# Hybrid encoder on one core: gate fills ahead of the attention units, and weights split in the projection

## The reference, cut to what matters

```
h = x @ W_in                        # one projection: q, k, v, gates of all branches, latents
A: causal attention with a forget term      logit[t,s] += F[t] - F[s]
B: window of 128 keys, one learned sink per head
C: keys and values from a normed latent     q = norm(cq) @ W_uq, k = ckv @ W_uk, v = ckv @ W_uv
branch_n = (attention_n * silu(gate_n)) @ W_br[n]            # "up"
m = sum over n of sigmoid(g_n) * branch_n                    # g = x @ W_in[:, 3072 gate columns]
x = LayerNorm(alpha * x + m @ W_o)
```

## Time and profile before

| | |
|---|---|
| median of the runs | 3636.93 us |
| profiled execution | 3634.75 us, of which the span is 3633.1 |
| TensorE busy | 3259.5 us, 90% |
| VectorE, ScalarE, GpSimd busy | 40%, 25%, 5% |
| granted TensorE clock, mean | 0.961 of full speed |
| DMA, mean | 116 GB/s |

### The profile page before, as it was taken

How to read it: one execution, slowest core, us unless ns; L and a number is a source line. 1 busy time by engine, 2 the same in 40 slices (tenths; PEclk the granted TensorE clock), 3 DMA queues, 4 the chain that set the end, 5 groups by cost and what they waited for, 6 DMA issues and landing times. The chain is left out here.

```text
span 3633.1 us, 52418 instructions
## 1 busy us (share of the span) xinstructions
PE 3259.5 (90%) x20718; PEld 2656.5 (73%) x20718; DVE 1466.5 (40%) x3367; ACT 896.6 (25%) x2006; POOL 172.6 (5%) x118
## 2 busy tenths in 40 slices
PE   0999986999999997988969999779999999977988
PEld 0788886777777775667858888767787777745867
DVE  5214234444444442354631143444434444423556
ACT  0221212333223332220121212223332233322110
POOL 0000000100110100000000000010111110000000
PEclk9999998999999998989979999889999999987999
DMA  5322216322333216764342222352223232096633
GB/s 197 110 87 94 84 54 201 86 69 59 88 93 88 83 39 173 228 234 151 127 157 89 91 96 68 115 158 68 69 72 91 85 94 66 30 262 205 217 136 110
DMA packets 405163, 419.73 MB, mean 116 GB/s; under 512 B 154561, under 2 KB 314177, under 8 KB 402561
## 3 DMA queue, kind: packets, MB, share of 16 engines
q1 hardware_dynamic: 371088, 376.87, 33.5%
q10 hardware_dynamic: 33840, 39.66, 3.3%
HBM read 291.17 MB, written 127.64 MB: 115 GB/s over the span
## 5 line engine op out<-in xcount | busy, mean ns | idle before, releaser
L351 PE MATMUL proj_acc<-proj_wh,keep_xh 128*128 128x512 f32 (+1 forms) x1296 | 501.7, 387 | 12.5 <-DVE proj_wl L326 12.5
L1066 PE MATMUL att_gacc<-att_gwh,keep_xh 128*128 128x256 f32 x1728 | 504.6, 292 | 2.5 <-POOL att_gwl L986 2.5
L352 PE MATMUL proj_acc<-proj_wl,keep_xh 128*128 128x512 f32 (+1 forms) x1296 | 500.4, 386 | 0.0
L353 PE MATMUL proj_acc<-proj_wh,keep_xl 128*128 128x512 f32 (+1 forms) x1296 | 500.2, 386 | 0.0
L1068 PE MATMUL att_gacc<-att_gwh,keep_xl 128*128 128x256 f32 x1728 | 486.8, 282 | 0.0
L1067 PE MATMUL att_gacc<-att_gwl,keep_xh 128*128 128x256 f32 x1728 | 485.9, 281 | 0.0
L1150 DVE COPY att_pt<-att_tr 128x256 f32<-128x256 f32 (+3 forms) x384 | 177.2, 461 | 620.9 <-PE att_tr L1031 620.6
L1093 ACT ACTIVATE att_p<-att_ss,att_stat 128x257 f32<-128x257 f32 (+9 forms) x384 | 249.4, 650 | 691.5 <-DVE att_stat L1143 691.5
L1020 PE MATMUL att_ss<-att_kt,att_qt 64*128 64x256 f32 (+9 forms) x1024 | 376.2, 469 | 1.3 <-DVE att_kt L1078 1.3
L1066 PEld LDWEIGHTS att_gacc<-att_gwh,keep_xh 128*128 128x128 f32 x1728 | 326.5, 189 | 17.2 <-issue 10.6
L1067 PEld LDWEIGHTS att_gacc<-att_gwl,keep_xh 128*128 128x128 f32 x1728 | 326.2, 189 | 0.0
(11 more groups left out here) (294 smaller groups left out, 4393.5 us busy)
## 6 DMA issues: line engine op xcount, KB each, us to landing
scratch_gates<-att_gout SPq DMA_DIRECT2D x216, 128.0 KB, 1.7
up_gates<-scratch_gates SPq DMA_DIRECT2D x18, 1536.0 KB, 8.0
proj_raw<-in_w_in SPq DMA_DIRECT2D x48, 512.0 KB, 3.7
att_graw<-in_w_in SPq DMA_DIRECT2D x48, 512.0 KB, 3.7
str_ka<-in_cache_a_kT SPq DMA_DIRECT2D x16, 1024.0 KB, 9.7
str_va<-in_cache_a_v SPq DMA_DIRECT2D x16, 1024.0 KB, 5.4
scratch_sg<-proj_out SPq DMA_DIRECT2D x54, 256.0 KB, 2.0
att_sg<-scratch_sg SPq DMA_DIRECT2D x24, 512.0 KB, 6.0
```

The lines of the kernel that those rows point to most:

```text
L351: nc.tensor.matmul(bank, hi, wh[:, u, kt, 0:w], start=kt == 0, stop=False)
L352: nc.tensor.matmul(bank, hi, wl[:, u, kt, 0:w], start=False, stop=False)
L353: mm = nc.tensor.matmul(bank, lo, wh[:, u, kt, 0:w], start=False, stop=kt == KT - 1)
L1066: nc.tensor.matmul(gacc[:, 0:GW], hi, gwh[:, n % 2, k, :], start=k == 0, stop=False)
```

## The change

The split weights of gate group 0 are made in the projection stage and kept (`keep_gw0`); its fills 0 to 3 are formed at the opening of the latent stage; the list of all fills runs on in one sequence, so fills 4 to 6 of group 0 open the attention, and units 0 to 6 have no fill at sub 13. A kept tile `early` of three row tiles serves in turn the x rows (ring of three), the raw gate weights, the position tables, `wq`, and the first rows of the up weights. The four row tiles of the attention's first unit are loaded in the latent stage, into a kept tile `row`.

```diff
+GW = 256
+EARLY_FILLS = 4
 # projections
-    XA = 4
+    XA = EARLIEST            # 3
+    graw = [C["early"][:, half, :] ... for half in range(2)]
 # SyncE, over the chunks c
+                if c in (1, 2):
+                    sp.dma_start(graw[half], w_src[... O_GATE:O_GATE + GW]).then_inc(gw_loaded, 16)
+                if c == 3:
+                    sp.wait_ge(gw_lo, 2)
+                    sp.dma_start(rope, ...); sp.dma_start(ropec, ...)
 # GpSimd
+            pool.wait_ge(x_taken, 2 * NT)
+            for half in range(2):
+                pool.wait_ge(gw_loaded, 16 * (half + 1))
+                nc.gpsimd.tensor_copy(hi, graw[half]).then_inc(gw_hi, 1)
+                nc.gpsimd.tensor_tensor(lo, graw[half], hi.bitcast(F32), ALU.subtract).then_inc(gw_lo, 1)
 # ScalarE
-            act.dma_start(rope[:], ...)
-            act.dma_start(ropec[:], ...)
 # latent_keys, SyncE, behind the first latent rows and wq
+            for i in range(RING):
+                sp.dma_start(C["row"][:, i, :, 0:HD], ...).then_inc(first_loaded, 16)
+            for t in range(EARLY_FILLS):
+                sp.wait_ge(g_taken, t + 1)
+                sp.dma_start(S["gates"][rows(t), 0:GW], gout[:, t, :]).then_inc(g_stored, 16)
 # TensorE, ahead of turn(0)
+            for t in range(EARLY_FILLS):
+                for k in range(KT):
+                    ...  # three matmuls into gacc[t]
 # ScalarE
+            take_gates(range(2))
+            act.wait_ge(wq_loaded, 16)
+            for raw, hi, lo in splits[:KQ]: ...
+            take_gates(range(2, EARLY_FILLS))
             take_turned(0)
 # VectorE
-            low_turned(0)
             for i, (raw, hi, lo) in enumerate(splits):
+                if i == KQ:
+                    low_turned(0)
 # attention_order
-    fills = [2, 3, 4, 5, 6, 8, 10, 12, 13]
+    fills = [(n, t) for n in range(len(UNITS)) for t in range(NT)][EARLY_FILLS:]
+    order = [("fill", *fills.pop(0)) for _ in range(3)] + order
+    places = [2, 3, 4, 5, 6, 8, 10, 12, 13]
+    spare = EARLY_FILLS + 3
-            if m in fills:
-                order.append(("fill", n, fills.index(m)))
+            if m in (places[:-1] if n < spare else places):
+                order.append(("fill", *fills.pop(0)))
 # prompt_attention, SyncE
-            load_row(0) ... load_gate(0, 0) ... load_gate(0, 1)
+            load_gate(1, 0) ... load_gate(1, 1)
+            sp.dma_start(C["early"][:], w_br_tiles(T, l)[:, 0:EARLIEST, :]).then_inc(early_loaded, 16)
-                    if t == 0 and n + 1 < len(UNITS):
+                    if t == 0 and 1 <= n and n + 1 < len(UNITS):
                         load_gate(n + 1, 0)
-                    if t == NT - 1 and n + 1 < len(UNITS):
+                    if t == NT - 1 and 1 <= n and n + 1 < len(UNITS):
                         load_gate(n + 1, 1)
 # the gate tiles sgr and sgt have one buffer each, before two
```

More of the change, by code:

```diff
@@ L256, in projections @@
     gkv = ph.sb("gkv", [P, KR])
-    XA = 4
-    xrow = ph.sb("xrow", [P, XA, D])
+    XA = EARLIEST
+    xrow = C["early"]
+    flat = C["early"][:].rearrange("p k n -> p (k n)")
+    rope = flat[:, 0:NT * 128].rearrange("p (t c) -> p t c", t=NT)
+    ropec = flat[:, NT * 128:NT * 192].rearrange("p (t c) -> p t c", t=NT)
+    graw = [C["early"][:, half, :].rearrange("p (k n) -> p k n", k=KT // 2) for half in range(2)]
+    gw_loaded, gw_hi, gw_lo = ph.sem("gw_loaded"), ph.sem("gw_hi"), ph.sem("gw_lo")
     x_loaded, x_taken = ph.ring("x_loaded", XA), ph.sem("x_taken")
@@ L327, in split_lo, with _ @@
                                     wh[:, u, kt, 0:w].bitcast(F32), ALU.subtract).then_inc(w_ready[u], 1)
+        @block.gpsimd
+        def _(pool):
+            pool.wait_ge(x_taken, 2 * NT)
+            for half in range(2):
+                hi, lo = (C["gw0"][:, r, 4 * half:4 * half + 4] for r in range(2))
+                pool.wait_ge(gw_loaded, 16 * (half + 1))
+                nc.gpsimd.tensor_copy(hi, graw[half]).then_inc(gw_hi, 1)
+                pool.wait_ge(gw_hi, half + 1)
+                nc.gpsimd.tensor_tensor(lo, graw[half], hi.bitcast(F32), ALU.subtract).then_inc(gw_lo, 1)
+            pool.wait_ge(gw_lo, 2)
         @block.tensor
@@ L577, in latent_keys @@
         ph.sem(n) for n in ("q_taken", "q_out", "k_taken", "k_out", "v_out"))
-    stored = ph.ring("stored", 2)
+    stored, first_loaded = ph.ring("stored", 2), ph.sem("first_loaded")
     HQ = H // 2
@@ L657, in forget_sums @@
                 mm.then_inc(sums_made, 1)
+            for t in range(EARLY_FILLS):
+                for k in range(KT):
+                    hi, lo = (x[:, k, rows(t)] for x in (C["xh"], C["xl"]))
+                    wh, wl = (C["gw0"][:, r, k, :] for r in range(2))
+                    nc.tensor.matmul(gacc[t], hi, wh, start=k == 0, stop=False)
+                    nc.tensor.matmul(gacc[t], hi, wl, start=False, stop=False)
+                    mm = nc.tensor.matmul(gacc[t], lo, wh, start=False, stop=k == KT - 1)
+                mm.then_inc(g_made, 1)
             turn(0)
@@ L826, in attention_order @@
     order += [("gate", len(UNITS) - 1, PT - 1), ("mix", len(UNITS) - 1, PT - 1)]
+    assert not fills
     return order
@@ L862, in prompt_attention, with gate_weights, fill_of @@
     g_made, g_taken, g_stored = ph.sem("g_made"), ph.sem("g_taken"), ph.ring("g_stored", 3)
+    def gate_weights(n):
+        return ((C["gw0"], gw1)[n % 2][:, r] for r in range(2))
+    def fill_of(n, t):
+        return NT * n + t - EARLY_FILLS
     groups = {}
@@ L970, in _ @@
             for part in range(3):
-                sp.wait_ge(g_stored[part], 16 * 3 * len(UNITS))
+                sp.wait_ge(g_stored[part], 16 * len(range(EARLY_FILLS + (part - EARLY_FILLS) % 3, NT * len(UNITS), 3)))
         @block.gpsimd
@@ L1309, in _ @@
                 load_c(n)
[L1310 removed]
+            sp.dma_start(C["early2"][:], w_br_tiles(T, l)[:, EARLIEST:EARLY, :]).then_inc(early_loaded, 16)
             def place(name, tile, h, wanted):
@@ L1711, in stream_attention, with early_tile @@
     ph.end()
-EARLY = 6
+EARLIEST, EARLY = 3, 6
+def early_tile(C, k):
+    return C["early"][:, k, :] if k < EARLIEST else C["early2"][:, k - EARLIEST, :]
 def w_br_tiles(T, l):
@@ L1732, in up_projection @@
     raw = ph.sb("raw", [P, 3, D])
-    early = C["early"]
     brt = ph.sb("brt", [P, 2, KB, P])
@@ L1752, in raw_tile @@
     def raw_tile(k):
-        return early[:, k, :] if k < EARLY else raw[:, (k - EARLY) % 3, :]
+        return early_tile(C, k) if k < EARLY else raw[:, (k - EARLY) % 3, :]
     def channels(tile, t, g):
@@ L1918, in raw_tile @@
     def raw_tile(k):
-        return C["early"][:, k, :] if k < EARLY else raw[:, k - EARLY, :]
+        return early_tile(C, k) if k < EARLY else raw[:, k - EARLY, :]
     def x_rows(t):
```

132 lines of the change are left out of this document (74 added, 58 removed).

## The result

| | before | changed |
|---|---|---|
| median of 5 runs | 3636.59 us | 3663.39 us (3655.86 to 3668.48) |
| ratio, 95% interval | | 1.0069 (1.0055 to 1.0083) |
| span of the profiled execution | 3633.1 us | 3662.5 us |
| granted clock, mean | 0.961 | 0.959 |

What follows compares the result with a forecast made beforehand. TensorE, busy 90% of the span, was taken as the bound. Per layer -5.8 - 1.0 - 20.3 + 26.0 + 6.9 = +5.8 us, +11.6 in all, gave 3648 us; range 3638 to 3659, with rivals 3630 to 3667.

Steps and rivals of the forecast that it cites:

- Line 3: Attention groups 0 to 6 lose the fill at sub 13, seven fills of 2.9 us: -20.3 us per layer.
- Part 4: Five weight-group borders now inside units: TensorE waits for the next group's load and split, +26.0 us per layer.
- Part 1: Projection opening: first product 9.1 us earlier, less 0.8 for a turn and 2.5 for a stall: -5.8 us per layer.
- Part 2: Openings of latent stage and attention: seven fills fit into TensorE's waits there, -1.0 us per layer.
- part 5: Slow clock after the four border waits over 4 us, 1.73 us each: +6.9 us per layer.
- The clock did not hold: Rival: clock holds through the border waits, part 5 is 0; -1.1 us per layer, 3635 us; chance 0.20.
- The half group did not land sooner: Rival: half group's load lands sooner mid-unit, shortening border waits; -4.9 us per layer, 3627 us; chance 0.12.
- the third rival: Projection opening bound by its weights, +1.9 instead of -5.8 us; +13.5 us per layer, 3664 us; chance 0.18.

Runs made afterwards that it cites:

- run 8: Changed kernel with a gate group's first half loaded behind fill (n, 2) instead of (n, 0), second behind (n, 6) instead of (n, 8): 3577.23 us, ratio 0.9837.
- Run 1: Changed kernel with the second half of a gate group loaded behind the store of fill (n, 3) instead of (n, 8): 3591.92 us, ratio 0.9867.
- Run 7: Kernel before, with only the position tables issued by SyncE ahead of the fourth chunk, ring of four kept: 3622.71 us, ratio 0.9958.
- run 4: Changed kernel with second half behind fill (n, 3) and the second chunk's weight loads ahead of x rows 6 to 8: 3582.28 us, ratio 0.9844.
- Run 2: Changed kernel with unread products added on TensorE to fill the six border waits, weights as late as before: 3642.21 us, ratio 1.0004.

## Why the prediction came out as it did

| per layer, us | forecast | layer 0 | layer 1 |
|---|---|---|---|
| 1: first product | -9.1 | -9.98 | -11.42 |
| 1: rest of the projection | +3.3 | +2.44 | +3.98 |
| 2: latent stage, attention opening | -1.0 | -1.60 | -1.64 |
| 3: seven fills | -20.3 | -20.3 | -20.3 |
| 4: border waits | +26.0 | +25.67 | +25.02 |
| 4: border 7 to 8 | 0 | +0.29 | +0.32 |
| 5: clock, by what is left of the units | +6.9 | +14.5 | +21.5 |

Line 3 is the forecast, carried over; the units with no border in them bear it out (unit 0 of the changed kernel -2.93 in layer 0, units 1 to 3 of run 8 near -2.85 each). The columns add up to +11.0 and +17.5, 28.5 of the 29.4 us between the two profiled spans.

**Right.** Part 4, which decides the sign: the waits are 7.11, 5.64, 2.67, 4.72 and 5.53, against 6.8, 5.9, 2.9, 4.7 and 5.6 forecast from gaps between tanhs of the old trace. Run 1 shows that they hang on the place of that load. Part 1: ScalarE's issue fell from 10.86 to 0.36 us, the first product came at 85.98 (86.9 forecast), and the seventh turn waited 1.95 (2.5). Run 7 shows the first half of that by itself, run 4 the second. Part 2: less the 7.54 us that the projection had gained by then, the fills were forecast from 534.5 to 547.8, the query products at 550.3 and the attention's first turn near 633.3; they came at 534.50, 548.23, 550.21 and 632.71.

**Wrong in size.** The step that failed is part 5, "I charge it for the four waits over 4 us and not for the one of 2.9: 4 x 1.73". The price was right: the fills behind these four waits took 7.3 us longer per layer than the 3.21 at full clock, against 6.9. The count was not. The waits of 2.7 and 1.6 us were followed by a slow fill too, 3.0 us together, so that the six fills took 10.3 us (10.2 in layer 1) longer than at full clock, 1.3 to 2.4 each. The other 4.2 and 11.3 us of line 5 go with falls that follow no wait, a term that the prediction put at nothing: one in layer 0, three in layer 1, among them 13.6 us in unit 4. Three of these four stand behind the collision of gate multiply and split; the one in unit 0 of layer 1 (2430.4, 3.4 us) stays open. I had looked for the clock only where I had seen a wait. Run 2 gives back 11.9 and 17.4 of the 14.5 and 21.5; most of the remainder is that its weights came later (first product 9.2 after the tanh at the border 1 to 2, not 8.7; 1.6 and 3.2 us over the six borders of a layer).

**The rivals.** The clock did not hold. The half group did not land sooner (4.52 to 5.19 until GpSimd starts at the five borders of both layers, 4.70 in the earlier trace rows). The measured 3663 lies on the number of the third rival (3664, bound by the weights' load), but by luck: its mechanism is not there, since the first product was 10 us earlier.

The Trainium skill ("TensorE: Matmul & The Clock Gate", section "HAM oscillation — how this bites in real kernels") says that a wait for a transfer between bursts of matmuls drops the clock and that the next burst starts slow. The trace agrees for the long waits, 4.60 to 7.11 us, and shows the same behind 2.67 and 1.60 us, but not behind 1.31.

## What to carry to other kernels

Where work is shifted along a fixed order, look at what else is keyed to its old place: here a load was still triggered by the last piece of the group before, and the border had moved from between units into one. Price such a wait with the clock behind it, and count every wait, the short ones too. Look as well at what the moved work now runs beside: here GpSimd's split met VectorE's multiply at the end of a unit, and the clock fell there without any wait for weights. And read the issuing engine's own row before costing a moved transfer: here the issue behind it held its engine for 10.86 us.

## What the runs showed of the hardware

VectorE's gate multiply of two tiles in SBUF takes 0.29 us and up to 2.4 beside GpSimd's subtraction, and then ends 0.15 us behind it. The Trainium skill ("Trainium Architecture — The Big Picture", section "What this means for kernel authors") says that VectorE and GpSimd share a pair of ports which one of them holds alone; the rows agree. In run 1 a delay of 1.5 us on VectorE so stands ahead of 10.2 us of TensorE at half clock, which begin where TensorE had only turns, scores and value products to do.

The changed kernel's runs spread over 12.6 us; their mean granted clock goes from 0.960 in the fastest to 0.955 in the slowest, so the falls differ from run to run. The kernel before does the same: over 17 runs beside run 1 it took 3625.66 to 3654.05 us, at 0.963 and 0.954.
